# One of four dense token blocks gets its gate matrix from one-hot products in place of scatters

## The reference

```python
q = (xt @ w_query).reshape(t, PEER_HEADS, 2, PEER_HALF)
s = jnp.einsum('thpd,hpnd->thpn', q, sub_keys)
s_top, i_top = lax.top_k(s, PEER_TOPK)
cand = s_top[:, :, 0, :, None] + s_top[:, :, 1, None, :]      # per head 16 x 16 candidates
c_top, c_idx = lax.top_k(cand.reshape(t, PEER_HEADS, 256), PEER_TOPK)
expert = idx1 * PEER_KEYS + idx2        # two key numbers of 0..127 each
gate = jax.nn.softmax(c_top, axis=-1)
hid = gelu(einsum('td,thkd->thk', xb, u_table[expert])) * gate
out = einsum('thk,thkd->td', hid, v_table[expert])
```

## Time and profile before

| | |
|---|---|
| median of three runs | 3674.01 us (3672.59 to 3676.25) |
| profiled execution, its own time | 3676.73 us |
| its span | 3675.0 us, mean granted TensorE clock 0.956 |
| PE busy | 3377.6 us (92%) |
| DVE busy | 2663.1 us (72%) |
| ACT busy | 926.6 us (25%) |
| POOL busy | 2061.8 us (56%) |
| scatters (L1420) | 512, 834.5 us busy, mean 1630 ns |
| DMA, mean over the span | 236 GB/s |

### The profile page before, as it was taken

The page is one execution under the profiler, slowest core; times in us unless marked ns, Lnnn a source line. Parts: engine busy times, 40 slices in busy tenths (PEclk is TensorE's granted clock), DMA queues, the critical chain, the costliest instruction groups (busy, mean ns, idle before and its releaser), DMA issues.

```text
span 3675.0 us, 36366 instructions
## 1 busy us (share of the span) xinstructions
PE 3377.6 (92%) x10816; PEld 1902.7 (52%) x10816; DVE 2663.1 (72%) x6220; ACT 926.6 (25%) x2312; POOL 2061.8 (56%) x1618
## 2 busy tenths in 40 slices
PE   7999997995998899495699999999999999999998
PEld 4666774574565677352244444444444444444443
DVE  2476664385798787324388889878988888888888
ACT  3244443211233344221011121112112121112212
POOL 1000000087888788788566666656665666565665
PEclk9999997997998899697799999999999999999999
DMA  4454113144432333342799999999999999999998
GB/s 122 155 205 162 58 39 131 49 104 82 69 53 24 52 53 36 79 86 6 258 400 384 390 394 375 379 358 397 376 375 394 388 387 375 386 387 380 371 408 326
DMA packets 370772, 868.60 MB, mean 236 GB/s; under 512 B 97552, under 2 KB 192016, under 8 KB 363408
## 3 DMA queue, kind: packets, MB, share of 16 engines
q0 software_dynamic: 221184, 537.23, 43.2%
q1 hardware_dynamic: 126976, 243.06, 18.2%
q10 hardware_dynamic: 22416, 85.99, 5.9%
HBM read 828.14 MB, written 38.01 MB: 236 GB/s over the span
## 4 chain that ended last, share of the span: by engine, by line
PE 48%; DMA 2%; DVE 1%; issue 1%; POOL 0%; ACT 0%; ACTq 0%; DVEq 0%; POOLq 0%
PE peer_ps_o L2053 24%; PE peer_ps_d L2040 21%; PE peer_ps_q L2003 2%; DMA peer_vr<-in_v_rows,index_g 1%; DMA peer_ur<-in_u_rows,index_g 0%; DVE Y L2201 0%; PE peer_ps_s L2013 0%; POOL peer_ur L1970 0%; DVE peer_ur L2190 0%; POOL peer_vr L1978 0%; DVE Y L2218 0%; PE peer_ps_t L2022 0%; DVE Y L2177 0%; ACT xg L2077 0%; DVE wk L2218 0%
## 5 line engine op out<-in xcount | busy, mean ns | idle before, releaser
L1420 POOL DMA_INDIRECT sel<-lists x512 | 834.5, 1630 | 290.1 <-issue 152.5
L1970 POOL DMA_INDIRECT peer_ur<-in_u_rows,index_g x512 | 566.6, 1107 | 519.6 <-DVE peer_ur L2190 396.0
L2201 DVE SCALAR_TENSOR_TENSOR Y<-peer_vr,osq,Y 128x1024 f32<-128x1024 f32 x512 | 657.1, 1283 | 93.5 <-DMA peer_vr<-in_v_rows,index_g 93.2
L1978 POOL DMA_INDIRECT peer_vr<-in_v_rows,index_g x512 | 599.1, 1170 | 195.7 <-issue 148.7
L2190 DVE SCALAR_TENSOR_TENSOR peer_ur<-peer_ur,Y 128x1024 f32<-128x1024 f32 x512 | 629.6, 1230 | 93.5 <-DMA peer_ur<-in_u_rows,index_g 93.5
L2053 PE MATMUL peer_ps_o<-hw,Y 128*128 128x512 f32 x1024 | 447.9, 597 | 8.4 <-DVE Y L2177 8.4
L2053 PE MATMUL peer_ps_o<-hnT,Y 128*128 128x512 f32 x1024 | 442.6, 592 | 0.0
L2040 PE MATMUL peer_ps_d<-hnT,state 128*128 128x512 f32 x688 | 303.9, 595 | 78.0 <-PEq L1455 78.0
L2053 PEld LDWEIGHTS peer_ps_o<-hw,Y 128*128 128x128 f32 x1024 | 196.1, 192 | 251.5 <-issue 238.9
L2053 PEld LDWEIGHTS peer_ps_o<-hnT,Y 128*128 128x128 f32 x1024 | 193.6, 190 | 238.7 <-issue 238.7
L2040 PE MATMUL peer_ps_d<-hnT,held 128*128 128x512 f32 x688 | 302.4, 592 | 0.7 <-ACT Y L2083 0.7
(11 more groups left out here) (335 smaller groups left out, 4910.3 us busy)
## 6 DMA issues: line engine op xcount, KB each, us to landing
sel<-Y ACTq DMA_DIRECT2D x16, 2048.0 KB, 7.0
peer_mt<-sel ACTq DMA_DIRECT2D x64, 512.0 KB, 7.6
hw<-in_v_cols SPq DMA_DIRECT2D x16, 2048.0 KB, 10.4
hnT<-in_v_cols SPq DMA_DIRECT2D x16, 2048.0 KB, 13.2
state<-in_u_cols SPq DMA_DIRECT2D x43, 512.0 KB, 7.1
held<-in_u_cols SPq DMA_DIRECT2D x43, 512.0 KB, 7.3
peer_ut<-in_u_cols SPq DMA_DIRECT2D x42, 512.0 KB, 7.3
w_group<-in_w_ssd SPq DMA_DIRECT2D x32, 512.0 KB, 4.1
```

Source lines behind the costliest of these rows:

```text
L1420: nc.gpsimd.indirect_dma_start(sel.rearrange("a i q two (t o) -> (a i q two t) o", o=1), bass.IndirectOffsetOnAxis(ap=R.index_d[:, at, k:k ...
L1970: nc.gpsimd.indirect_dma_start(ur[:, r % RING, :], None, u_rows, bass.IndirectOffsetOnAxis(ap=R.index_g[:, r // TOPK % RQ, r % TOPK:r % TO ...
L1978: nc.gpsimd.indirect_dma_start(vr[:, r % RING, :], None, v_rows, bass.IndirectOffsetOnAxis(ap=R.index_g[:, r // TOPK % RQ, r % TOPK:r % TO ...
L2201: nc.vector.scalar_tensor_tensor(out=hb, in0=vr[:, s, :], scalar=hid[:, c:c + 1], in1=hb, op0=ALU.mult, op1=ALU.add).then_inc(comb_done, 1)
```

## The change

Blocks 0 to 2 are scattered as before (24 units, 384 scatters). For block 3 (units 17, 19, ... 31, `BUILT`) `route_place` stores the chosen expert numbers, and in front of the loop `peer()` builds that quarter of `sel`. The numbers are split into first and second key and transposed together with the gates. For each token two 128x128 matrices are formed whose rows are the token's 128 choices: A has a one where the column is the choice's first key, B the gate where it is the second key. A turned times B is the token's 128x128 matrix of gates. Four tokens make a group, 32 groups in all. VectorE makes A for the four tokens (`hot`, one comparison) and B for three of them; ScalarE makes the fourth token's B (`hot_last`: gate minus gate times the absolute difference, cut at zero). TensorE does four products into one PSUM bank, and ScalarE copies the bank in two halves of 128x256 (`place_out`) to four staging tiles of 2 MB that lie in tiles which the loop uses later; the read steps through PSUM with the tokens innermost, so its elements are 128 words apart, and the write has runs of four words. A and B are two deep, as are the PSUM banks. SP stores the first two tiles after group 15 and the last two after group 31, in runs of 512 bytes. TensorE starts the loop when all is staged; the first GELU, the first gathers of `v` and ScalarE's loads of `sel` wait for the stores.

The core of the diff:

```diff
-DENSE = [n for n in range(UNITS) if n // (2 * PH) * 2 + n % 2 < DB]
+SCATTERED = [n for n in range(UNITS) if n // (2 * PH) * 2 + n % 2 < DB - 1]
+BUILT = [n for n in range(UNITS) if n // (2 * PH) * 2 + n % 2 == DB - 1]
+DENSE = SCATTERED + BUILT
...
-SCATTER_MIX0, SCATTER_PROLOGUE, SCATTER_SSD = DENSE[0:5], DENSE[5:8], DENSE[8:15]
-SCATTER_CHUNK = 7
-SCATTER_HG, SCATTER_MIX1 = DENSE[15:25], DENSE[25:]
+SCATTER_MIX0, SCATTER_PROLOGUE, SCATTER_SSD = SCATTERED[0:4], SCATTERED[4:7], SCATTERED[7:12]
+SCATTER_CHUNK = 5
+SCATTER_HG, SCATTER_MIX1 = SCATTERED[12:20], SCATTERED[20:]
+M_GROUPS = P // 4
+PER_BATCH = SELB // 4
...
+    if n in BUILT:
+        nc.vector.tensor_copy(R.built_key[:, BUILT.index(n) * TOPK:(BUILT.index(n) + 1) * TOPK], chosen
+                              ).then_inc(R.routed, 1)
+        return
...
+            for x in range(4):
+                batch, hh, parts = x // 2, x % 2, stage_parts(x)
+                sp.wait_ge(staged, 2 * (PER_BATCH * (batch + 1) - 1) + hh + 1)
...
+            sp.wait_ge(sel_out[0], sel_stores(0))
             sp.dma_start(va, v_cols[0, 0]).then_inc(v_in[0], 16)
...
+            pool.wait_ge(sel_out[1], sel_stores(1))
             for r in range(RING):
                 v_row(r)
...
+            for j in range(M_GROUPS):
+                pe.wait_ge(hot_ready, 2 * (j + 1))
+                pe.wait_ge(last_ready, 2 * (j + 1))
+                need(pe, staged, 2 * (j - 1))
+                for q in range(4):
+                    mm = nc.tensor.matmul(ps_o[:, j % 2, q * P:(q + 1) * P], hot_a[j % 2][:, q, :], hot_b[j % 2][:, q, :],
+                                          start=True, stop=True)
+                mm.then_inc(sel_made, 1)
+            pe.wait_ge(staged, 2 * M_GROUPS)
...
+            def hot_last(j):
+                t = j * 4 + 3
...
+                nc.scalar.activation(to, count, ACT.Abs, scale=-1.0, bias=pickedT[:, 1, t:t + 1]).then_inc(last_ready, 1)
+                act.wait_ge(last_ready, 2 * j + 1)
+                nc.scalar.activation(to, to, ACT.Relu, scale=pickedT[:, 3, t:t + 1],
+                                     bias=pickedT[:, 2, t:t + 1]).then_inc(last_ready, 1)
+
+            def place_out(j, hh):
...
+                source = ps_o[:, j % 2, :].rearrange("p (q i) -> p q i", q=4)[:, :, hh * 64:(hh + 1) * 64]
...
+                    nc.scalar.activation(to.rearrange("p b (i t) -> p (b i) t", t=SELB)[:, :, t:t + 4],
+                                         source.rearrange("p q i -> p i q"), ACT.Copy).then_inc(staged, 1)
...
             def gelu(e):
                 act.wait_ge(s_made, e + 1)
+                if e == 0:
+                    act.wait_ge(sel_out[1], sel_stores(1))
...
+            for j in range(M_GROUPS):
+                place_out(j, 0)
+                if j + 2 < M_GROUPS:
+                    hot_last(j + 2)
+                place_out(j, 1)
...
+            def hot(j):
...
+                need(dve, sel_made, j - 1)
+                t = j * 4
+                nc.vector.tensor_tensor(hot_a[j % 2], count.unsqueeze(1).to_broadcast([P, 4, KEYS]),
+                                        pickedT[:, 0, t:t + 4].unsqueeze(2).to_broadcast([P, 4, KEYS]),
+                                        ALU.is_equal).then_inc(hot_ready, 1)
+                for q in range(3):
+                    ins = nc.vector.tensor_scalar(hot_b[j % 2][:, q, :], count, pickedT[:, 1, t + q:t + q + 1],
+                                                  pickedT[:, 2, t + q:t + q + 1], ALU.is_equal, ALU.mult)
+                ins.then_inc(hot_ready, 1)
```

More of the change, by code:

```diff
@@ L1892, in peer @@
         fw_in = sem("fw_in")
+        split_done, pick_turned, pick_out = sem("split_done"), sem("pick_turned"), sem("pick_out")
+        hot_ready, sel_made, staged, last_ready = sem("hot_ready"), sem("sel_made"), sem("staged"), sem("last_ready")
+        sel_out = [sem(f"sel_out{i}") for i in range(2)]
         x_turned, x_out = sem("x_turned"), sem("x_out")
@@ L1981, in v_row @@
                                              ).then_inc(got_v[r % RING], 16)
+            nc.gpsimd.iota(count_u, pattern=[[1, KEYS]], base=0, channel_multiplier=0).then_inc(M.counted, 1)
             for r in range(RING):
                 u_row(r)
+            pool.wait_ge(sel_out[1], sel_stores(1))
             for r in range(RING):
@@ L2219, in norm @@
                                                op0=ALU.mult, op1=ALU.mult).then_inc(f_normed, 1)
-            for b in range(DB):
+            def hot(j):
+                if j == 0:
+                    dve.wait_ge(pick_out, 1)
+                need(dve, sel_made, j - 1)
[7 more added lines that the diff above has]
+                ins.then_inc(hot_ready, 1)
+            own = R.own
+            own.now(nc.vector.tensor_scalar(first_u, R.built_key, 1.0 / KEYS, 0.5 / KEYS - 0.5, ALU.mult, ALU.add))
+            own.now(nc.vector.tensor_copy(first_key, first_u))
+            nc.vector.scalar_tensor_tensor(out=R.built_key, in0=first_key, scalar=-float(KEYS), in1=R.built_key,
+                                           op0=ALU.mult, op1=ALU.add).then_inc(split_done, 1)
+            dve.wait_ge(M.counted, 2)
+            nc.vector.tensor_copy(count, count_u).then_inc(split_done, 1)
+            dve.wait_ge(split_done, 2)
+            for j in range(M_GROUPS):
+                hot(j)
+            for b in range(DB - 1):
                 dve.wait_ge(R.scattered[b], 16 * TOPK * PH)
@@ L2290, in block_program @@
                     hnT, R, ut)
-        peer(nc, w_route, u_cols, v_cols, u_rows, v_rows, fin_w, sel, C, Y, osq, hw, hnT, R, ut, out)
+        peer(nc, M, w_route, u_cols, v_cols, u_rows, v_rows, fin_w, sel, C, Y, osq, hw, hnT, R, ut, out)
 def laid_out(inputs):
```

51 lines of the change are left out of this document (48 added, 3 removed).

## The result

| | before | after |
|---|---|---|
| median of the timed runs (us) | 3673.30 (3672.4 to 3676.25, 4 runs) | 3586.43 (3577.88 to 3591.81, 4 runs) |
| ratio after to before | | 0.976, 95% interval 0.9739 to 0.9781 |
| profiled execution, its span (us) | 3675.0 | 3576.1 |
| TensorE clock over the span | 0.956 | 0.975 |
| PE busy | 3377.6 us (92%) | 3398.0 us (95%) |

The profiled execution of after is the fastest of its four, so against the one of before it shows 99 us.

The account below looks back on a forecast made before the run. TensorE's dense products bound the loop, and POOL's scatters end stages before it. Shorter stages -122, build start-up +4, groups +50 and stores +3 sum to -65: 3609 us by the median (3611.7 profiled), range 3590 to 3644.

Parts of the forecast that it names:

- -20.6: First output projection: with 16 fewer scatters POOL ends before VectorE, so the stage ends with VectorE, 20.6 us sooner.
- -28: Second HGRN2 stage: with 32 fewer scatters POOL ends before VectorE despite three landing waits, saving 28 us.
- -60.4: Second output projection: with 48 fewer scatters and three landing waits POOL ends before VectorE, saving 60.4 us.
- Nothing but scatters runs: Before the dense loop, only POOL's scatters run for 60.4 us after VectorE's last instruction of the second projection.
- The SSD stage, 3 + 10 = -13: Second SSD stage: five scatters a chunk, not seven, save 3 us in the first eight chunks, 10 in the last eight.
- VectorE saves five small operations per unit ... left out: Fourth-block units: five VectorE operations saved, under 1 us each, three units in the HGRN2 stage; not counted in the sum.
- The build, +4 and 1.5 a group: Build before the loop: start-up +4 us, then 32 groups at 1.5 us set by VectorE or ScalarE, +50.
- plus a little for the hand-overs: Build: a group costs what its slowest engine needs plus a little for hand-overs, 1.5 us at full clock.
- The stores, +3: Last two stores into `sel` take 16 us, delaying the first GELU past two dense products: +3 us, 0 to 8.
- Rival A: TensorE's clock stays at half through the build, which takes 62 us in place of 50; 3621 us, chance 0.13.
- Rival B: ScalarE's strided PSUM evictions in the build are dear, 87 us in place of 50; 3646 us, chance 0.10.
- Rival C: Build groups don't overlap, 4.7 us each, 150 in all; 3709 us, chance 0.04.

Follow-up runs that it names:

- before_again: The kernel before the change, run again without an edit; 3672.37 us.
- before_b: The kernel before the change, run a third time without an edit; 3669.42 us.
- again: The changed kernel once more, no edit but one constant written another way with the same value; 3583.59 us.
- again_b: The changed kernel once more, as yardstick for two versions run beside it; 3585.95 us.
- five_ops: Changed kernel with the four small VectorE operations per fourth-block unit that the change left out run again, results unused; two executions, 3582.00 and 3582.99 us.
- one_deep: Changed kernel, but VectorE starts a build group's operands only when TensorE has finished the group before; 3650.29 us.
- deal_hg: Changed kernel with ten units (160 scatters) in the second HGRN2 stage and two in the second projection; run twice, 3630.17 and 3630.52 us.
- pool_two: Changed kernel with POOL making two of each build group's four B matrices, VectorE two, ScalarE none; 3603.70 us.
- split_alt: Changed kernel with a semaphore per staging tile's store, one B matrix per group on POOL and ScalarE's on every other group; 3588.09 us.

## Why the prediction came out too slow

The means of three profiles each (before, before_again, before_b; after, again, again_b) leave less to chance. Per stage, from first instruction to first instruction (the first row is the point at which the second SSD stage starts):

| us | before | after | difference | predicted |
|---|---|---|---|---|
| start of the second SSD stage | 889.1 | 865.7 | -23.4 | -20.6 |
| second SSD stage | 333.0 | 320.2 | -12.8 | -13 |
| second HGRN2 stage | 321.1 | 284.5 | -36.6 | -28 |
| second projection | 231.9 | 165.2 | -66.7 | -60.4 |
| barrier to first dense product | 0 | 50.5 | +50.5 | +54 |
| first dense product to the end | 1895.9 | 1895.3 | -0.6 | +3 |
| sum | | | -89.6 | -65 |

- **"Nothing but scatters runs", 128 fewer, the stages end with VectorE:** right at all three boundaries.
- **The SSD stage, 3 + 10 = -13:** right, to 0.2 us, and in its parts too: by TensorE's first product of each chunk the first eight give 2.7 us and the rest 10. In the first eight `awide` stands some 13.5 us apart and POOL waits before it for TensorE, as "what is late next" had it.
- **The step that failed: "-20.6", "-28" and "-60.4" were counted from POOL's last scatter to VectorE's last instruction**, as if the next stage began at the end of whichever engine is last. The row that closes the interval was in the trace: TensorE at 1779.76 against 1773.40. Behind a scatter on POOL it begins 3.7 to 6.5 us later (13 boundaries in seven profiles), because POOL's DRAIN outlasts the scatter; behind VectorE it begins 0.3 to 0.6 later. Three boundaries make 14 us of the 24.6 that the sum is off. (The first row of the table hides some of it: the executions of after reached the first projection 1.6 us later on the mean, and that stage itself is 25.0 us shorter.)
- **"VectorE saves five small operations per unit ... left out":** five go and one comes, so they are four. The HGRN2 stage's own work fell from 288.9 to 283.9 on the mean. Over it the granted clock was 0.92, 0.93 and 0.92 in before and 0.94, 0.93 and 0.93 in the changed kernel; length times what is missing to 1.00 gives, as an estimate, 22.7 us against 18.5, so some 4 of the 5.0 us are TensorE's clock. The same estimate is 19.9 for both executions of five_ops and 19.5 for again: these operations bring one fall back, but what makes the rest of the difference is not explained.
- **The build, +4 and 1.5 a group:** right in kind, 4 us too dear. The start-up to the first product was 4.2 and the groups, past the first three at half clock, 1.36 to 1.42, VectorE's busy time and nothing on top; the "plus a little for the hand-overs" was not there, because VectorE did not wait again after its first four groups.
- **The stores, +3:** they took 16.8 us, the prediction 16; it left out ScalarE's 2.9 us behind them, and the two products before them took 14.0 us, not 15.7. The stall was 7 us, at the product that the prediction named, but the first group became only 1.4 us longer on the mean, and a group near the end was 1.9 us shorter, so the way from the first product to the end is no longer than before. The prediction took a stall at the start as paid. What ends the first group's wait is VectorE, and TensorE's own half-clock start (8.63 us, now 7.13), its wait (3.67, now 1.55) and the half-clock products behind that wait (23.42, now 21.73) shrank in exchange. The last in the kernel before:

```profile
1853.93 23.42 PE L2053 MATMUL peer_ps_o<-hw,Y 128*128 128x512 f32 x50 [3.67 <-DVE Y L2177]
```

- **Rival A (clock):** out. TensorE stands 0.23 to 0.29 us between groups, and the clock, 0.50 for 8 us, is 1.00 from 10 us behind the barrier on. The Trainium skill ("TensorE: Matmul & The Clock Gate", section "A second HAM failure mode: psum-queue depth-cycling") describes a swing with brief idling between banks; this trace does not show it here. In one_deep, where TensorE stands 1.56 us ahead of each 2.08, the clock stayed at its lower level (0.50), 1.2 GHz.
- **Rival B (strided evictions):** out. An element every 512 bytes costs what a contiguous one costs, 0.36 to 0.38 against 0.385. The forecast took the contiguous price without a row for it; the measurement bears it out. The Trainium skill ("Advanced Engine Details and Errata", section "Memory Cachelines") has a penalty for SBUF accesses that each take a new line, and for PSUM says that patterns that are not contiguous slow matmuls; for ScalarE's reads of 128x256 from PSUM this trace shows no penalty.
- **Rival C (no overlap):** its point of decision, 3.6 us a group, is what one_deep has (3.63). That version is still faster than before, 3650 against 3673, by the gain that the prediction did not count. **Rival D:** out.

The range failed because each of its ends was made of the bounds of the build, the stores and the SSD stage. The three large terms had none, as if read off. (Its lower end is also 2 us off as a sum: 3609 - 6 - 7 - 3 = 3593, not 3591.)

## What to carry to other kernels

Where an engine that issues scatters ends a stage, count its cost to the first instruction of the next stage, not to its own last one, and look at its DRAIN, which the page does not count as busy. Where TensorE no longer stands ahead of a stage, look at its clock there too (8.63 us for the loop's first product after 78 us of standing, 7.13 right behind the build), and where a stall is added, for one further on that it replaces. A term that is read off the trace needs an error too: three executions of the same program started the loop anywhere from 1630 to 1641 us, while from there to the end they agreed within 0.5.

## What the runs showed of the hardware that was not expected

- A stage boundary at which POOL is last costs 3.1 us after short iotas and 3.7 to 6.5 after scatters (0.3 to 0.6 with VectorE last); a DRAIN on POOL's sequencer fills this time. At the HGRN2 stage's end it was 3.70 in three executions of the kernel before and 6.47 in both of deal_hg.
- The last scatter had landed 1.60 us after its instruction ended on POOL; the boundary did not wait for it.
- A compare and multiply with two scalars on 128x128 f32 takes POOL 0.93 us on the mean in pool_two and 1.34 in split_alt, VectorE 0.28.
- In pool_two TensorE stands 0.60 to 0.63 us ahead of each 1.13 and the clock reads 1.00; in one_deep it stands 1.56 ahead of each 2.08 and the clock reads 0.50.
